# Full 128x128 stationary tiles in two attention cores and in the choice of keys

## The chip, the cores and the metric

The kernel runs on one core of one Trainium2 chip. The metric is the device time of one execution in microseconds (us). A core has TensorE (PE; its weight loads are shown apart as PEld), VectorE (DVE), ScalarE (ACT), GpSimd (POOL) and SyncE (SP), which issues most transfers. Each engine works through its own list of instructions in order and waits on semaphores for the others.

## The reference, cut to what matters

Two transformer blocks run over 512 positions of width 1024. The change lies in the second block, in its two attention branches:

```
z = h @ w_in
a_q, a_k, a_v, i_q, i_k, i_w, c_q, c_kv, k_r, g = split_cols(z, IN_SIZES)

# branch A: sparse attention, 8 heads of width 64, one key and one value shared by all heads
dots  = einsum('bqhd,bsd->bqhs', iq, ik) * 64 ** -0.5          # 4 indexer heads of width 64
score = einsum('bqh,bqhs->bqs', iw, relu(dots))                # causal
sel   = top_k(score, 128)
p     = softmax(q @ k_sel * 64 ** -0.5 + bias)                 # over the chosen keys
y_a   = p @ v_sel

# branch B: 8 heads, query and key of width 64 + 32 (rope), value of width 64
logits = (qn . kn + qr . kr) * 96 ** -0.5                      # causal
y_b    = softmax(logits) @ v
```

Queries are taken in blocks of 128 positions (qb = 0 to 3), which see 128 (qb + 1) keys.

## The kernel before, in words

A matrix product on PE takes a stationary tile (contraction rows on partitions x output rows) and a moving one. Most products are split: weights and activations are each held as a high and a low part, and `mm3` (L288) issues high x high, high x low and low x high. The products of the attention cores are plain float products through `mm` (L293), and each is carried out as two passes, which the trace shows as two weight loads and two matmuls (x2). The profile gives a stationary tile as rows*columns: 64*128, 96*128, 128*64 or 128*128.

The changed stage is `branch_stage` (from L1944). In order on PE:

- The input products z (`z_ch` weights) for 8 tiles, then the sparse queries `AQ`, then the gates (`gt`). A generator, `best_pe`, is advanced from within these products. It turns the token values (`tokens`) and issues the indexer's score products `dots`, one for each of 4 heads and each of qb = 1 to 3 (qb = 0 sees only 128 keys and needs no choice). The indexer's queries `IQ` and key `IK` lie in slots of the tile `QM`: two heads share one 128-partition tile, so head h uses partitions 64 (h % 2) to 64 (h % 2) + 63, and the key is there twice, once for each half. `best_dve` adds up the weighted scores and finds the 128 largest in 16 rounds of `max` and `match_replace` for every qb; the result is `Msel`, a bf16 mask.
- The values of branch B, `VB` (a 128x512 tile for each block of 128 keys, 64 columns a head).
- The MLA core: 32 items (8 heads, 4 query blocks). Before a pair of heads, `heads_pe` makes the pair's queries and keys, which ACT copies and DVE turns (rope) into `QM` and `KM`.
- The DSA core: 32 items (4 query blocks, 8 heads), with the output products of branch B (`branch_b_pe`) advanced by one step for each item, from the third item on, 24 steps in all.

Both cores are objects of the class `Core`. Item i passes `scores` (PE: in the DSA core first a mask product, identity x `Msel`, then query x key), `soft` (DVE: bias and row maximum), `exps` (ACT), `weigh` (DVE), `turns` (PE: transposes of 128x128, L816), `turned` (ACT: copy to `sq`) and `values` (PE: values as the stationary tile, 128 keys x 64 columns, over `sq`). `Core.run` sets a fixed order: in one step every engine works on its parts of different items, on PE `scores(i)`, `turns(i - 3)`, `values(i - 4)`. The output of a value product lies in partitions 0 to 63 of a PSUM bank; `mla_close_act` and `dsa_close_act` copy it to the lower or upper half of a pair tile.

On POOL the stage has only the powers for norms: `power("z")`, `power("cq")`, `power("ckv")`. PE's `spread` products wait for them. DVE's `z_evac` scales the z tiles out of PSUM; tile 6 holds the sparse key `AK`, once in each half of the partitions.

Of the kernel before, what the change touches and what calls it, by code (L numbers as in the profile page):

```python
# [214 lines left out]
def program(nc, ins, out):  # L215
# [3 lines left out]
    with ctx:  # L219
# [1724 lines left out]
        def branch_stage():  # L1944
            QOFF = [0, 128, 384, 768]
            ph = ExitStack()
            GT, Msel = sb("GT", [P, 16, S], F32, ph), sb("Msel", [P, 1280], BF16, ph)
            identb = sb("identb", [P, P], BF16, ph)
            AK, AV = sb("AK", [P, S], F32, ph), sb("AV", [P, 4, 64], F32, ph)
            AQ, IW = sb("AQ", [P, 4, S], F32, ph), sb("IW", [P, 4, 4], F32, ph)  # L1950
            SC = [sb(f"sc{i}", [P, S], F32, ph) for i in range(2)]
            pm = ExitStack()
            QM, KM, VB = sb("QM", [P, 4, S], F32, pm), sb("KM", [P, 4, S], F32, pm), sb("VB", [P, 4, S], F32, pm)
# [5 lines left out]
            stat_a = sb("stat_a", [P, 8 * 4 * 3], F32, pa)  # L1959
            pa.close()  # L1960
            B2.insert(0, sb("B20", [P, 2, H, 64], F32, pa))
            pa.close()
# [7 lines left out]
            stat_b, mx8 = extra[:, 0:96], [extra[:, 96:104], extra[:, 104:112]]  # L1970
# [45 lines left out]
            def best_pe():  # L2016
                for _ in range(3):
                    yield
                b = acc_bank("tokens", [(act_done, "tokens")])
                pe.wait_ge(*dve_done["zt", 7])  # L2020
                for tb in range(4):
                    tok = pe.e.transpose(b[:, tb * P:(tb + 1) * P], tmp[3][:, tb * P:(tb + 1) * P], ident[:, :])
                tok.then_inc(*core_done.up("tokens"))
                yield
                for qb in range(1, 4):
                    N = P * (qb + 1)
                    for h in range(4):
                        rows = slice(64 * (h % 2), 64 * (h % 2) + 64)
# [65 lines left out]
            def mla_item(h, qb):  # L2094
                N, x, j = P * (qb + 1), 2 * ((h // 2) % 2) + h % 2, h // 2
                b = OB["mla"][h % 2]
                return {"N": N, "in1": causal[:, S - N:S], "in1_ready": lambda: [pool_done["causal"]], "scale": 96.0 ** -0.5,
                        "comps": [(QM[0:96, x, qb * P:(qb + 1) * P], KM[0:96, x, 0:N])],
                        "ready": lambda: [act_done["mq", j, h % 2], dve_done["mrot", j, h % 2], act_done["kr"], act_done["mk", j, h % 2]],
                        "v": lambda kb: (VB[:, kb, 64 * h:64 * h + 64], act_done["vb", 3]), "bank": b,  # L2100
                        "dest": banks[b][0:64, qb * P:(qb + 1) * P], "opens": (act_done, ("mo", h)) if qb == 0 else None}

            def dsa_item(h, qb):
                N, n = P * (qb + 1), 2 * qb + h // 4
                rows = slice(64 * (h % 2), 64 * (h % 2) + 64)
# [136 lines left out]
            def mla_close_act(i):  # L2242
                if i and i % 8 == 0:
                    split_b_act(i // 8 - 1)
                if i % 4 == 3:
                    h = i // 4
                    act.wait_ge(*core_done["mla", "V", i])
                    if h // 2 > 1:
                        act.wait_ge(*dve_done["yb", h // 2 - 2])
                    act.e.activation(pair_buf[h // 2 % 2][64 * (h % 2):64 * (h % 2) + 64, :], banks[OB["mla"][h % 2]][0:64, :],  # L2250
                                     ACT.Copy).then_inc(*act_done.up(("mo", h)))

            def mla_close_dve(i):
                if i and i % 8 == 0:
# [17 lines left out]
            def dsa_close_act(i):  # L2272
                if i and i % 4 == 0:
                    split_a_act(i // 4 - 1)
                if i % 4 == 3:
                    n = i // 4
                    o = split_a(n)[2]
                    from_ = banks[OB["dsa"][n % 2]][:, :].rearrange("p (j x q) -> p j x q", j=2, x=2)
                    act.wait_ge(*core_done["dsa", "V", i])
                    act.wait_ge(*(dve_done["ya", n - 2] if n > 1 else dve_done["yb", 3]))  # L2280
                    act.e.activation(o[0:64], from_[0:64, :, 0, :], ACT.Copy).then_inc(*act_done.up())
                    act.e.activation(o[64:P], from_[0:64, :, 1, :], ACT.Copy).then_inc(*act_done.up(("do", n)))

            def dsa_close_dve(i):
                if i and i % 4 == 0:
# [39 lines left out]
                     lambda m: [(dve_done, ("x", "f2", m))])  # L2325


            def times_norm(dst, b, *key):
                dve.wait_ge(*act_done["rb", "z"])
                dve.e.tensor_tensor(dst, b[:, :], RB, ALU.mult).then_inc(*dve_done.up(key))  # L2330

            def z_evac(m):
                dve.wait_ge(*gemm_done["z", m])
                dst = [CQ[:, 0, :], CQ[:, 1, :], CQ[:, 2, :], tmp[0][:, :], IQ[:, 0, :], IQ[:, 1, :], AK[:, :], tmp[3][:, :]][m]
                times_norm(dst, bank(("z", m)), "zt", m)
# [4 lines left out]
            def vector():  # L2340
# [11 lines left out]

                def aq_evac(m):
                    dve.wait_ge(*gemm_done["aq", m])
                    times_norm(AQ[:, m, :], bank(("aq", m)), "aq", m)

                beside_gemm(dve, "z_ch", 0, DT, 2, aq_evac)
                dve.within[:] = [top]
# [1 line left out]

                def gt_evac(m):
                    dve.wait_ge(*gemm_done["gt", m])
                    times_norm(GT[:, m, :], bank(("gt", m)), "gt", m)

                beside_gemm(dve, "gates", 0, DT, 8, gt_evac)
                dve.within[:] = []
# [33 lines left out]
            def z_act(m):  # L2400
                if m == 3:
                    act.wait_ge(*dve_done["zt", 3])
                    act.e.activation(IK[0:64, :], tmp[0][0:64, :], ACT.Copy).then_inc(*act_done.up())
                    act.e.activation(IK[64:P, :], tmp[0][0:64, :], ACT.Copy).then_inc(*act_done.up("ik"))
# [284 lines left out]
```

## Time and profile before

| | |
|---|---|
| median of 3 runs | 2220.16 us (2215.21 to 2221.14) |
| span of the profiled execution | 2216.4 us |
| PE busy | 2123.1 us, 96% |
| weight loads (PEld) | 1654.6 us, 75% |
| DVE busy | 1344.6 us, 61% |
| ACT busy | 870.1 us, 39% |
| POOL busy | 154.3 us, 7% |

The profiled execution is one run; its span is counted from its first to its last instruction, and the run's own device time is not given apart from the three above. The span lies 3.8 us below their median. Busy time of PE is the union of its matmuls' modelled durations, so that matmuls following one another closely overlap, and a busy PE is not PE at its peak.

### The profile page before, as it was taken

What the parts mean: (1) busy time and instruction counts of PE and PEld (TensorE: products, weight loads), DVE (VectorE), ACT (ScalarE), POOL (GpSimd) and SP (SyncE); (2) the same over time, 40 slices, a digit from 0 to 9 for tenths busy, and PEclk for the clock granted to TensorE, in tenths of its full rate; (3) what the DMA queues carried; (4) which work ended last, traced back from release to release, by engine and by line L of the source; (5) the groups of instructions that cost most, each with busy time, mean ns of one, the idle gap of its engine ahead of it and who ended that gap; (6) DMA issues with size and microseconds to landing.
All of it is one profiled execution on the core that took longest, in us unless ns stands there. A gap on an engine that the chain in (4) does not pass through costs nothing.

```text
span 2216.4 us, 26169 instructions
## 1 busy us (share of the span) xinstructions
PE 2123.1 (96%) x10573; PEld 1654.6 (75%) x10575; DVE 1344.6 (61%) x2281; ACT 870.1 (39%) x1453; POOL 154.3 (7%) x101
## 2 busy tenths in 40 slices
PE   5999999999999999899999999999989999999998
PEld 4755768888887876677887887776755588888886
DVE  7697478847834566647764566458775465623632
ACT  4455534423423255534432443332365433412421
POOL 0464100000010000020000001000000000000000
PEclk9999999999999999999999999999999999999998
DMA  8343226565521221012333233222113022332331
GB/s 304 126 148 99 77 67 202 189 208 172 181 92 58 77 67 39 29 48 82 103 107 106 90 95 120 67 76 77 49 47 124 20 80 91 95 96 94 95 95 67
DMA packets 67112, 225.01 MB, mean 102 GB/s; under 512 B 7216, under 2 KB 8112, under 8 KB 66992
## 3 DMA queue, kind: packets, MB, share of 16 engines
q1 hardware_dynamic: 64112, 218.11, 30.6%
q10 hardware_dynamic: 2880, 5.24, 0.6%
q8 instruction: 83, 1.36, 0.3%
q14 instruction: 37, 0.30, 0.0%
HBM read 215.98 MB, written 7.34 MB: 101 GB/s over the span
## 4 chain that ended last, share of the span: by engine, by line
PE 84%; DVE 9%; ACT 3%; issue 2%; DMA 0%; POOL 0%; SPq 0%; DVEq 0%; POOLq 0%; ACTq 0%
PE bank L289 23%; PE bank L291 22%; PE bank L290 22%; PE bank L294 15%; PE bank L816 1%; DVE wlo L329 1%; ACT whi L316 1%; DVE sc L2084 1%; DVE steps L2082 1%; DVE tmp L545 1%; DVE Hl L550 1%; ACT pr L789 1%; DVE pr L781 0%; POOL small L525 0%; DMA XT<-in_xT 0%
## 5 line engine op out<-in xcount | busy, mean ns | idle before, releaser
L289 PE MATMUL bank<-Hh,whi 128*128 128x512 f32 x1632 | 653.8, 401 | 25.2 <-DVE wlo L329 9.9
L290 PE MATMUL bank<-Hl,whi 128*128 128x512 f32 x1632 | 640.4, 392 | 0.0
L291 PE MATMUL bank<-Hh,wlo 128*128 128x512 f32 x1632 | 640.4, 392 | 0.0
L329 DVE TENSOR_TENSOR wlo<-stg,whi 128x1024 fp32r<-128x1024 f32 (+1 forms) x299 | 358.8, 1205 | 427.6 <-ACT whi L316 427.0
L316 ACT ACTIVATE whi<-stg 128x1024 fp32r<-128x1024 f32 (+1 forms) x309 | 313.1, 1025 | 424.9 <-PE bank L291 418.3
L289 PEld LDWEIGHTS bank<-Hh,whi 128*128 128x128 f32 x1632 | 309.6, 190 | 105.6 <-issue 19.4
L291 PEld LDWEIGHTS bank<-Hh,wlo 128*128 128x128 f32 x1632 | 309.4, 190 | 66.0
L290 PEld LDWEIGHTS bank<-Hl,whi 128*128 128x128 f32 x1632 | 310.1, 190 | 61.0 <-issue 0.2
L289 PE MATMUL bank<-HIDh,whi 128*128 128x512 f32 x352 | 141.9, 403 | 0.0
L291 PE MATMUL bank<-HIDh,wlo 128*128 128x512 f32 x352 | 140.0, 398 | 0.0
L290 PE MATMUL bank<-HIDl,whi 128*128 128x512 f32 x352 | 138.6, 394 | 0.0
L1111 DVE SCALAR_TENSOR_TENSOR bank<-U,vec,bank 128x512 f32<-128x512 f32 x145 | 109.6, 756 | 5.1
L432 POOL TENSOR_TENSOR part<-sq 128x512 f32<-128x512 f32 x7 | 9.0, 1291 | 1357.3 <-ACT sq L427 1339.8
L291 PE MATMUL bank<-HID2h,wlo 128*128 128x512 f32 x256 | 102.1, 399 | 0.0
L290 PE MATMUL bank<-HID2l,whi 128*128 128x512 f32 x256 | 100.9, 394 | 0.0
L289 PE MATMUL bank<-HID2h,whi 128*128 128x512 f32 x256 | 100.5, 393 | 0.0
L1446 DVE SCALAR_TENSOR_TENSOR tmp<-bank,vec,tmp 128x511 f32<-128x511 f32 x88 | 65.9, 748 | 49.1 <-ACT tmp L1400 49.1
L629 DVE CUSTOM_DVE_ANT_0 raw<-raw,c_act 128x1024 f32<-128x1024 f32 x72 | 87.2, 1219 | 5.8 <-DMA raw<-in_mod_w 5.6
L1400 ACT ACTIVATE tmp<-bank,vec 128x512 f32<-128x512 f32 x88 | 67.7, 770 | 55.0 <-PE bank L291 55.0
L294 PE MATMUL bank<-U,dtap 128*128 128x512 f32 x186 | 85.1, 616 | 1.2 <-ACT dtap L1251 1.2
L291 PEld LDWEIGHTS bank<-HIDh,wlo 128*128 128x128 f32 x352 | 66.1, 188 | 15.6
L290 PEld LDWEIGHTS bank<-HIDl,whi 128*128 128x128 f32 x352 | 66.2, 188 | 15.0
(296 smaller groups left out, 2757.0 us busy)
## 6 DMA issues: line engine op xcount, KB each, us to landing
raw<-in_mod_w SPq DMA_DIRECT2D x96, 512.0 KB, 4.4
stg<-in_ffn_in SPq DMA_DIRECT2D x88, 512.0 KB, 3.8
stg<-in_ff SPq DMA_DIRECT2D x64, 512.0 KB, 3.5
stg<-in_ffn_out SPq DMA_DIRECT2D x40, 512.0 KB, 3.6
stg<-in_cm_w SPq DMA_DIRECT2D x24, 512.0 KB, 3.8
stg<-in_gates SPq DMA_DIRECT2D x16, 512.0 KB, 3.5
stg<-in_z_ch SPq DMA_DIRECT2D x12, 512.0 KB, 3.6
bias_kept<-out_b ACTq DMA_DIRECT2D x20, 256.0 KB, 2.1
```

Source lines behind the costliest of these rows:

```text
L289: pe.e.matmul(out_, l[0], r[0], start=start, stop=False, skip_group_check=True)
L290: pe.e.matmul(out_, l[0], r[1], start=False, stop=False, skip_group_check=True)
L291: return pe.e.matmul(out_, l[1], r[0], start=False, stop=stop, skip_group_check=True)
L294: return pe.e.matmul(out_, l, r, start=start, stop=stop, skip_group_check=True)
L316: act.e.activation(whi[j % NW][:, 0:n * c], stg[j % NSTG][:, 0:n * c], ACT.Copy).then_inc(*w_hi.up(j))
L329: hand.e.tensor_tensor(wlo[j % NW][:, 0:n * c], stg[j % NSTG][:, 0:n * c], whi[j % NW][:, 0:n * c].bitcast(F32), ALU.subtract).then_inc(*m ...
L545: dve.e.scalar_tensor_tensor(tmp[t % 4][:, :], x_tile(t), gain, r[:, :], ALU.mult, ALU.mult).then_inc(*dve_done.up(("hm", ver, t)))
L550: dve.e.scalar_tensor_tensor(Hl[:, t, :], tmp[t % 4][:, :], shift, Hh[:, t, :].bitcast(F32), ALU.add, ALU.subtract).then_inc(*dve_done.up( ...
L629: dve.e.tensor_tensor_reduce(raw[j % NRAW][:, :], raw[j % NRAW][:, :], c_act[:, :], 1.0, 0.0, ALU.mult, ALU.add, modv[:, a:a + 1]).then_in ...
L1111: dve.e.scalar_tensor_tensor(a[:, :] if k < CONV - 1 else C[:, t, :], U[:, t, k:k + S], vcol("cm_dw", 8 * k + t), a[:, :], ALU.mult, ALU.a ...
L1400: act.e.activation(at_, bank((("up", l, j), m))[:, :], ACT.Identity, bias=column(bcol + c), scale=column(w3 + 88 + c)).then_inc(*act_done. ...
L1446: dve.e.scalar_tensor_tensor(o[:, 1:S], from_[:, 0:S - 1], column(w3 + 44 + c), o[:, 1:S], ALU.mult, ALU.add).then_inc(*dve_done.up())
```

## The change

All products of the two cores and of the indexer now have a stationary tile that fills the array's columns, and those with 64 contraction rows get 128. (The scores of the MLA core keep their 96 rows.)

- Keys. `IK` and `AK` each become two tiles, one for even and one for odd heads. The one for even heads has the key in partitions 0 to 63 and zeros in 64 to 127, the other the reverse. The product takes the whole 128-partition query tile with two heads in it; the zeros cancel the other head. POOL writes the four halves of zeros once, behind `power("z")`; the score products of indexer and DSA core wait for the last one.
- Values. In the MLA core the stationary tile holds the values of both heads of the pair (128 columns), in the DSA core the shared value twice. The output fills 128 partitions, of which the half that belongs to the head is copied.
- `z_evac(6)` writes its two halves into the two key tiles with two DVE operations in place of one; ACT copies the token values twice.
- The identity in bf16, the indexer's head weights `IW` and the statistics `stat_a` move into parts of an existing tile (`steps_t`).

```diff
-            AK, AV = sb("AK", [P, S], F32, ph), sb("AV", [P, 4, 64], F32, ph)
-            AQ, IW = sb("AQ", [P, 4, S], F32, ph), sb("IW", [P, 4, 4], F32, ph)
+            AK, AV = [sb(f"AK{x}", [P, S], F32, ph) for x in range(2)], sb("AV", [P, 4, P], F32, ph)
+            AQ = sb("AQ", [P, 4, S], F32, ph)
...
-            IQ, IK, CQ = QM[:, 0:2, :], QM[:, 2, :], VB
+            IQ, IK, CQ = QM[:, 0:2, :], [QM[:, 2, :], QM[:, 3, :]], VB
...
+                        pe.wait_ge(*pool_done["zeros"])
                         pe.wait_ge(*dve_done["zt", 5])
-                        mm(banks[5][:, 0:N], IQ[rows, h // 2, qb * P:(qb + 1) * P], IK[rows, 0:N], True, True).then_inc(
+                        mm(banks[5][:, 0:N], IQ[:, h // 2, qb * P:(qb + 1) * P], IK[h % 2][:, 0:N], True, True).then_inc(
...
-                act.e.activation(AV[:, :, :], from_[:, :, 0:64], ACT.Copy).then_inc(*act_done.up("av"))
+                act.e.activation(AV[:, :, 0:64], from_[:, :, 0:64], ACT.Copy).then_inc(*act_done.up())
+                act.e.activation(AV[:, :, 64:P], from_[:, :, 0:64], ACT.Copy).then_inc(*act_done.up("av"))
...
-                        "v": lambda kb: (VB[:, kb, 64 * h:64 * h + 64], act_done["vb", 3]), "bank": b,
-                        "dest": banks[b][0:64, qb * P:(qb + 1) * P], "opens": (act_done, ("mo", h)) if qb == 0 else None}
+                        "v": lambda kb: (VB[:, kb, P * j:P * j + P], act_done["vb", 3]), "bank": b,
+                        "dest": banks[b][:, qb * P:(qb + 1) * P], "opens": (act_done, ("mo", h)) if qb == 0 else None}
...
-                        "comps": [(AQ[rows, h // 2, qb * P:(qb + 1) * P], AK[rows, 0:N])],
-                        "ready": lambda: [dve_done["aq", h // 2], dve_done["zt", 6], dve_done["idb"]] + (
+                        "comps": [(AQ[:, h // 2, qb * P:(qb + 1) * P], AK[h % 2][:, 0:N])],
+                        "ready": lambda: [dve_done["aq", h // 2], dve_done["zt", 6], dve_done["idb"], pool_done["zeros"]] + (
...
-                        "dest": banks[b][0:64, (h % 4) * P:(h % 4 + 1) * P], "opens": (act_done, ("do", n)) if h % 4 == 0 else None}
+                        "dest": banks[b][:, (h % 4) * P:(h % 4 + 1) * P], "opens": (act_done, ("do", n)) if h % 4 == 0 else None}
...
+                if m == 6:
+                    times_norm(AK[0][0:64, :], bank(("z", m)), [], slice(0, 64))
+                    times_norm(AK[1][64:P, :], bank(("z", m)), [("zt", m)], slice(64, P))
+                    return
...
                 power("z")
                 pool.wait_ge(*norm_done["sum", "z"])
+                for x, other in ((0, slice(64, P)), (1, slice(0, 64))):
+                    pool.wait_ge(*pool_done.now)
+                    pool.e.memset(IK[x][other, :], 0.0).then_inc(*pool_done.up())
+                    pool.wait_ge(*pool_done.now)
+                    pool.e.memset(AK[x][other, :], 0.0).then_inc(*pool_done.up(*(["zeros"] if x else [])))
+                pool.wait_ge(*pool_done.now)
                 power("cq")
```

## Rows read from the trace of the kernel before

**Rows 1.** The chain of waits that ended last, by engine.

```profile
PE 84%; DVE 9%; ACT 3%; issue 2%; DMA 0%; POOL 0%; SPq 0%; DVEq 0%; POOLq 0%; ACTq 0%
```

**Rows 2.** By stretch: us; PE, PEld, DVE, ACT, POOL busy; clock; DMA.

```profile
1440.00:1475.00 35.00, 34.53 (x171) 28.91 (x170) 16.91 (x25) 11.11 (x16) 3.02 (x3) 0.95 0.24 73
1475.00:1517.00 42.00, 42.00 (x170) 30.16 (x169) 30.40 (x71) 13.63 (x21) 0.00 (x0) 1.00 0.24 77
1517.00:1600.00 83.00, 75.52 (x301) 57.88 (x300) 67.62 (x131) 21.05 (x28) 0.00 (x0) 0.94 0.19 59
1622.70:1641.55 18.85, 17.56 (x93) 11.71 (x93) 13.50 (x42) 12.76 (x34) 0.00 (x0) 1.00 0.18 57
1684.00:1780.00 96.00, 94.86 (x450) 56.58 (x452) 45.54 (x150) 45.05 (x127) 0.00 (x0) 1.00 0.18 61
```

**Rows 3.** Timeline of PE in the DSA core: start us, us, instructions merged.

```profile
1729.49 0.91 PE L294 MATMUL bank<-AK,AQ 64*128 64x384 f32 x2
1730.33 0.55 PE L816 MATMUL bank<-ident,sc 128*128 128x128 f32 x3
1730.81 0.65 PE L294 MATMUL bank<-sq,AV 128*64 128x128 f32 x4
1731.39 0.50 PE L289 MATMUL bank<-Hh,whi 128*128 128x512 f32 x1
...
1732.20 0.34 PE L294 MATMUL bank<-Msel,identb 128*128 128x384 bf16 x1
1732.46 0.91 PE L294 MATMUL bank<-AK,AQ 64*128 64x384 f32 x2
```

**Rows 4.** Timeline of PE in the MLA core.

```profile
1643.95 1.09 PE L294 MATMUL bank<-sq,VB 128*64 128x128 f32 x8
1644.96 0.49 PE L294 MATMUL bank<-KM,QM 96*128 96x128 f32 x2
1645.29 0.38 PE L816 MATMUL bank<-ident,sc 128*128 128x128 f32 x2
1645.60 0.43 PE L294 MATMUL bank<-sq,VB 128*64 128x128 f32 x2
```

**Rows 5.** Timeline of PE at the indexer's first product.

```profile
1476.35 0.70 PE L294 MATMUL bank<-QM 64*128 64x256 f32 x2
1476.98 0.50 PE L289 MATMUL bank<-Hh,whi 128*128 128x512 f32 x1
```

**Rows 6.** Timeline of PE in the first block's attention core, full value tiles.

```profile
814.97 0.52 PE L816 MATMUL bank<-ident,pr 128*128 128x128 f32 x3 [1.05 <-DVE pr L808]
815.32 0.61 PE L294 MATMUL bank<-aT,Vt 128*128 128x128 f32 x4
815.69 0.48 PE L289 MATMUL bank<-Hh,whi 128*128 128x512 f32 x1
816.00 0.39 PE L290 MATMUL bank<-Hl,whi 128*128 128x512 f32 x1
```

**Rows 7.** Groups by line: busy us, mean ns of one, idle before.

```profile
L294 PEld LDWEIGHTS bank<-aT,Vt 128*128 128x128 f32 x160 | 21.8, 202 | 0.1
...
L294 PEld LDWEIGHTS bank<-sq,AV 128*64 128x64 f32 x160 | 16.6, 136 | 4.9 <-issue 4.0
```

**Rows 8.** PE's waits in the MLA core: us in total, times, longest.

```profile
PE bank L289 <- ACT QM L2203: 1.0, 1, 1.0
```

**Rows 9.** Timeline of PE, bf16 products ahead of a split product.

```profile
1141.53 0.63 PE L294 MATMUL bank<-Tb,step 128*128 128x32 bf16 x19
1142.01 0.48 PE L289 MATMUL bank<-HIDh,whi 128*128 128x512 f32 x1
```

**Rows 10.** POOL at the cq power (timeline), and its additions (groups by line).

```profile
1456.81 1.01 POOL L525 TENSOR_TENSOR small<-small 128x4 f32<-128x4 f32 x1 [14.59 <-DVE small L505]
...
L436 POOL TENSOR_TENSOR part<-part,sq 128x512 f32<-128x512 f32 x28 | 38.4, 1370 | 126.4 <-ACT sq L427 123.6 <-ACT sq L1243 1.8
```

**Rows 11.** Timeline of PE in the first block, scores of two components.

```profile
821.36 0.92 PE L294 MATMUL bank<-Kt,Qt 64*128 64x384 f32 x4
```

More of the change, by code:

```diff
@@ L1947, in branch_stage @@
             GT, Msel = sb("GT", [P, 16, S], F32, ph), sb("Msel", [P, 1280], BF16, ph)
-            identb = sb("identb", [P, P], BF16, ph)
-            AK, AV = sb("AK", [P, S], F32, ph), sb("AV", [P, 4, 64], F32, ph)
-            AQ, IW = sb("AQ", [P, 4, S], F32, ph), sb("IW", [P, 4, 4], F32, ph)
+            AK, AV = [sb(f"AK{x}", [P, S], F32, ph) for x in range(2)], sb("AV", [P, 4, P], F32, ph)
+            AQ = sb("AQ", [P, 4, S], F32, ph)
             SC = [sb(f"sc{i}", [P, S], F32, ph) for i in range(2)]
@@ L1958, in branch_stage @@
             B2 = [sb(f"B2{qb}", [P, 2 * qb + 2, H, 64], F32, pa) for qb in (3, 2, 1)][::-1]
-            stat_a = sb("stat_a", [P, 8 * 4 * 3], F32, pa)
             pa.close()
@@ L1967, in branch_stage @@
             YBh, YBl, YAh, YAl = Hh[:, 0:4, :], Hl[:, 0:4, :], Hh[:, 4:8, :], Hl[:, 4:8, :]
-            IQ, IK, CQ = QM[:, 0:2, :], QM[:, 2, :], VB
+            IQ, IK, CQ = QM[:, 0:2, :], [QM[:, 2, :], QM[:, 3, :]], VB
             extra = steps_t[:, 2, :].bitcast(F32)
-            stat_b, mx8 = extra[:, 0:96], [extra[:, 96:104], extra[:, 104:112]]
+            stat_b, stat_a, mx8 = extra[:, 0:96], extra[:, 112:208], [extra[:, 96:104], extra[:, 104:112]]
+            identb, IW = steps_t[:, 3, 0:P], steps_t[:, 3, P:P + 32].bitcast(F32).rearrange("p (t h) -> p t h", t=4)
             RB = steps_t[:, 0:2, :].rearrange("p x q -> p (x q)").bitcast(F32)
@@ L2027, in best_pe @@
                     for h in range(4):
-                        rows = slice(64 * (h % 2), 64 * (h % 2) + 64)
                         open_bank(5, [(act_done, ("relu", qb, h))])
                         pe.wait_ge(*act_done["ik"])
+                        pe.wait_ge(*pool_done["zeros"])
                         pe.wait_ge(*dve_done["zt", 5])
-                        mm(banks[5][:, 0:N], IQ[rows, h // 2, qb * P:(qb + 1) * P], IK[rows, 0:N], True, True).then_inc(
+                        mm(banks[5][:, 0:N], IQ[:, h // 2, qb * P:(qb + 1) * P], IK[h % 2][:, 0:N], True, True).then_inc(
                             *core_done.up(("dots", qb, h)))
@@ L2099, in mla_item @@
                         "ready": lambda: [act_done["mq", j, h % 2], dve_done["mrot", j, h % 2], act_done["kr"], act_done["mk", j, h % 2]],
-                        "v": lambda kb: (VB[:, kb, 64 * h:64 * h + 64], act_done["vb", 3]), "bank": b,
-                        "dest": banks[b][0:64, qb * P:(qb + 1) * P], "opens": (act_done, ("mo", h)) if qb == 0 else None}
+                        "v": lambda kb: (VB[:, kb, P * j:P * j + P], act_done["vb", 3]), "bank": b,
+                        "dest": banks[b][:, qb * P:(qb + 1) * P], "opens": (act_done, ("mo", h)) if qb == 0 else None}
             def dsa_item(h, qb):
                 N, n = P * (qb + 1), 2 * qb + h // 4
-                rows = slice(64 * (h % 2), 64 * (h % 2) + 64)
                 b = OB["dsa"][n % 2]
@@ L2249, in mla_close_act @@
                         act.wait_ge(*dve_done["yb", h // 2 - 2])
-                    act.e.activation(pair_buf[h // 2 % 2][64 * (h % 2):64 * (h % 2) + 64, :], banks[OB["mla"][h % 2]][0:64, :],
-                                     ACT.Copy).then_inc(*act_done.up(("mo", h)))
+                    rows = slice(64 * (h % 2), 64 * (h % 2) + 64)
+                    act.e.activation(pair_buf[h // 2 % 2][rows, :], banks[OB["mla"][h % 2]][rows, :], ACT.Copy).then_inc(*act_done.up(("mo", h)))
             def mla_close_dve(i):
@@ L2281, in dsa_close_act @@
                     act.e.activation(o[0:64], from_[0:64, :, 0, :], ACT.Copy).then_inc(*act_done.up())
-                    act.e.activation(o[64:P], from_[0:64, :, 1, :], ACT.Copy).then_inc(*act_done.up(("do", n)))
+                    act.e.activation(o[64:P], from_[64:P, :, 1, :], ACT.Copy).then_inc(*act_done.up(("do", n)))
             def dsa_close_dve(i):
@@ L2325, in tensor, with times_norm @@
                      lambda m: [(dve_done, ("x", "f2", m))])
-            def times_norm(dst, b, *key):
+            def times_norm(dst, b, key, rows=slice(0, P)):
                 dve.wait_ge(*act_done["rb", "z"])
-                dve.e.tensor_tensor(dst, b[:, :], RB, ALU.mult).then_inc(*dve_done.up(key))
+                dve.e.tensor_tensor(dst, b[rows, :], RB[rows, :], ALU.mult).then_inc(*dve_done.up(*key))
             def z_evac(m):
                 dve.wait_ge(*gemm_done["z", m])
-                dst = [CQ[:, 0, :], CQ[:, 1, :], CQ[:, 2, :], tmp[0][:, :], IQ[:, 0, :], IQ[:, 1, :], AK[:, :], tmp[3][:, :]][m]
-                times_norm(dst, bank(("z", m)), "zt", m)
+                if m == 6:
+                    times_norm(AK[0][0:64, :], bank(("z", m)), [], slice(0, 64))
+                    times_norm(AK[1][64:P, :], bank(("z", m)), [("zt", m)], slice(64, P))
+                    return
+                dst = [CQ[:, 0, :], CQ[:, 1, :], CQ[:, 2, :], tmp[0][:, :], IQ[:, 0, :], IQ[:, 1, :], None, tmp[3][:, :]][m]
+                times_norm(dst, bank(("z", m)), [("zt", m)])
                 if m == 3:
@@ L2354, in aq_evac @@
                     dve.wait_ge(*gemm_done["aq", m])
-                    times_norm(AQ[:, m, :], bank(("aq", m)), "aq", m)
+                    times_norm(AQ[:, m, :], bank(("aq", m)), [("aq", m)])
                 beside_gemm(dve, "z_ch", 0, DT, 2, aq_evac)
@@ L2362, in gt_evac @@
                     dve.wait_ge(*gemm_done["gt", m])
-                    times_norm(GT[:, m, :], bank(("gt", m)), "gt", m)
+                    times_norm(GT[:, m, :], bank(("gt", m)), [("gt", m)])
                 beside_gemm(dve, "gates", 0, DT, 8, gt_evac)
@@ L2402, in z_act @@
                     act.wait_ge(*dve_done["zt", 3])
-                    act.e.activation(IK[0:64, :], tmp[0][0:64, :], ACT.Copy).then_inc(*act_done.up())
-                    act.e.activation(IK[64:P, :], tmp[0][0:64, :], ACT.Copy).then_inc(*act_done.up("ik"))
+                    act.e.activation(IK[0][0:64, :], tmp[0][0:64, :], ACT.Copy).then_inc(*act_done.up())
+                    act.e.activation(IK[1][64:P, :], tmp[0][0:64, :], ACT.Copy).then_inc(*act_done.up("ik"))
                     act.wait_ge(*dve_done["kr"])
```

## The prediction

> **What bounds the kernel now.** I read the page first, for the chain of waits, then busy time by stretch, then the timeline of TensorE alone in the stage that is changed, then the groups by line and the list of waits. The chain that ended last lies on PE for 84% [rows 1], so the first question of any edit is what it does to PE's order of work, and only the second what it does to the others. The stretches [rows 2] cut the changed stage into parts with different limits. From 1475 to 1517 us (second part of the input products, with eight of the indexer's score products among them) PE is busy 42.00 of 42.00 us. From 1517 to 1600 us DVE has 67.6 of 83 us and PE has holes: this is the choice of keys, where DVE's chain of maxima leads. One pair of heads of the MLA core, 1622.70 to 1641.55 us, has PE at 17.56 of 18.85 us, DVE at 13.50, ACT at 12.76. The sparse core (DSA), 1684 to 1780 us, has PE at 94.9 of 96 us, DVE and ACT at 45 each. [...]
>
> PE busy is not PE at work, because the ends of products are modelled, so I compare ends: the end of a row is its start plus its us, and the distance between two ends, less what the later products take in a dense stream, is time lost between them. Stream times: one pass of 128 columns takes 0.11 (value products x8 in 1.09, x2 in 0.43: six more in 0.66) [rows 4]; a 512-column pass of a split (high/low) product 0.22 to 0.23 (end 816.17 to end 816.39) [rows 6]; a float product is two passes at half that speed, 0.32 a pass at 384 columns and 0.43 at 512, in proportion to the 0.11 [rows 4].
>
> One item of the sparse core [rows 3]:
> - score (64 rows) to transposes: ends 1730.40 and 1730.88, 0.48 for three transposes of 0.11: lost 0.15.
> - transposes to values (64 columns): ends 1730.88 and 1731.46, 0.58 for four of 0.11: lost 0.14.
> - values to the first product of branch B: ends 1731.46 and 1731.89, 0.43 for 0.23: lost 0.20.
> - mask to score: ends 1732.54 and 1733.37, 0.83 for two passes of 0.32: lost 0.19.
>
> One item of the MLA core [rows 4]: values to the next score, ends 1645.04 and 1645.45, 0.41 for 0.22, lost 0.19. Score (96 rows) to transposes, ends 1645.45 and 1645.67, 0.22 for 0.22: nothing lost. Transposes to values, 1645.67 to 1646.03, 0.36 for 0.22: lost 0.14. The indexer [rows 5]: from the 64-row product back to the main products, ends 1477.05 and 1477.48, 0.43 for 0.23: lost 0.20.
>
> So time goes exactly where a stationary tile with 64 rows or 64 columns stands next to one that is full, and none where 96 rows meet 128. What full tiles do in the same place is shown by the first block's attention [rows 6]: transposes, then value products with a 128*128 tile, then split products end at 815.49, 815.93 and 816.17. That is 0.44 for four passes and 0.24 for one of 0.23: nothing is lost, though type and bank change too.
>
> **The change part by part.**
>
> *MLA values, 64 to 128 columns.* 32 items, each enters and leaves the 64-column tile once: 32 x (0.14 + 0.19) = 10.6 us of PE. The product itself: 0.44 for four at full width [rows 6] against 0.11 each at 64 columns [rows 4], so no charge. The weight load grows from 136 to 202 ns [rows 7]; beside a full product it stays covered, as the 0.1 us of idle time before the 160 full loads says. Lost again: with PE faster, what is late next? In one pair of heads PE streams scores 5 x 0.86 = 4.3 (2,560 columns, two passes), 20 transposes and 40 value passes at 0.11 = 6.6, and 15 head products at 0.23 = 3.5: 14.4 us, plus 8 x 0.33 = 2.6 lost at the tiles: 17.0 of 18.85. The remaining 1.8 are waits, among them one on the readers of the head products' bank [rows 8]. After the change DVE's 13.5 and ACT's 12.8 stand beside 14.4 rather than 17.0. The pair is still PE's, but DVE must also turn the new heads in one lump (six operations), and the order is fixed on every engine. I give back a quarter, 0.65 of 2.6 a pair: 8.0 us saved in the stage. Bounds: 10.6 (no new wait) and 1.5 (the pair falls only towards the floor of its waits, priced under the rivals).
>
> *DSA scores to 128 rows, values to 128 columns.* 32 items.
> - Mask to score: 0.19 each. What remains is a load of 128 columns behind a short mask product. The nearest row is a 32-column bf16 product before a full split product, ends 1142.16 and 1142.49, 0.33 for 0.23 [rows 9]: 0.10 stays. With 128 columns of mask (8 items) I let 0.06 stay, else 0.02: 8 x 0.13 + 24 x 0.17 = 5.1. Bounds: 2.9 (0.10 stays everywhere) and 6.1.
> - Score to transposes: 32 x 0.15 = 4.8, less a few thousandths each: 4.6.
> - Transposes to values: 32 x 0.14 = 4.5.
> - Values to branch B, which stands behind 24 of the items: 24 x 0.19 = 4.6. The other 8 go on to a mask; no row here separates that step, it lies between 0 and 0.2, I take 0.1: 0.8.
>
> Sum 19.6. DVE and ACT have over 40% free even in 76 us; I give back 0.8 for odd waits: 18.8. Bounds 15 and 21.
>
> *Indexer scores to 128 rows.* 12 products, each with an exit of 0.20 and an entry priced as mask to score, 0.19. The first 8 lie in the stretch where PE has no hole: 8 x 0.39 = 3.1. The last 4 lie where DVE leads: 0, at best 1.6.
>
> *Costs.* The padding needs four POOL writes of 64x512. They stand behind the z power and ahead of the cq power, before which POOL idles 14.59 us [rows 10]. The trace has no such write; the nearest POOL row, a 128x512 addition, takes 1.37: four make 5.5 us, and even with a semaphore between them they end near 1449, before the power at 1456.8 and long before the first indexer product at 1476 that waits for them. Cost 0; it begins above 3.3 us a write, and then PE's spread product is late, with the input products behind it. The evacuation of z tile 6 becomes two on DVE, at a place where DVE is busy 16.9 of 35 us [rows 2]; ACT, with 13.6 of 42 busy, copies the token values once more, ahead of a weight split and of the first relu. I bound each from above by the larger POOL addition, 1.37 [rows 10], and take 0 for both. The added waits on the zeros stand in PE's queue ahead of products that also wait for later events. Moving the identity, the head weights and the statistics to other memory changes no instruction.
>
> [...] In the first block's attention four 64-row passes of 384 columns end in 0.92 us [rows 11], while in the sparse core two such passes take 0.91 [rows 3]: there two components in different row halves run at the same time, here each score stands alone between mask and transposes. [...]
>
> **Sum.** 8.0 + 18.8 + 3.1 = 29.9 us, off the profiled execution's span of 2216.4: 2186.5. The median of the runs is 2220.16, 3.8 above that span, so 2190.
>
> **Rivals.**
> 1. *The MLA core becomes bound by its helpers* (0.12). The head preparation, ACT's copy, DVE's turn, then PE's third product in the same bank, sets the pair's length, and only some 0.2 a pair is won there. For: a wait on the bank's readers is in the list already [rows 8], and DVE's load is 13.5. Against: 14.4 + 1.8 of waits is still above 13.5. Then 18.8 + 3.1 + 0.7 = 22.6: 2197.6.
> 2. *The step from mask to score stays* because the type changes as well as the tile (0.06). For: mask to score is the one changed step with a type change into a float product. Against: 0.10 at 32 columns [rows 9]. Then 29.9 - 5.1: 2195.4.
> 3. *The other side: wide loads aren't covered* (0.03). If each of the 320 value loads stood in the open with its 0.20 [rows 7] behind a product of only 0.11, 64 us would come and 30 go: 2220 + 34 = 2254. It decides for slower from 0.10 a load. Against: the full-width value products of the first block stream at 0.11 [rows 6].
> 4. *The change doesn't do what it says* (0.03): the loss belongs to the order of operations and not to the tile, and stays. Then 2220. Against: rows 6 have the same order without loss.
>
> **How the numbers follow.** Forecast 0.76, rivals 0.12, 0.06, 0.03, 0.03. A difference of 0.3% (6.7 us) is what can be told from none. Faster: 0.76 + 0.12 + 0.06 = 0.94; same 0.03 (rival 4); slower 0.03 (rival 3). Low end: all of 10.6 + 21 + 4 = 35.6, 2184.6, with 1.6 for the runs' spread: 2183. High end: rival 1 with its 2197.6 and a further 4 (bounds of the DSA sum): 2202. That leaves out some 0.15.
>
> **What would show it.** Right: DSA shrinks from 96 to about 77 us; a pair of heads from 18.85 to about 16.8; 1475 to 1517 to about 39; value loads near 200 ns at unchanged ends of 0.11 a pass; no idle time before loads of the value and score groups; the stages before and behind unchanged. Wrong: a pair of heads above 18; ends between value passes above 0.13; losses of 0.15 or more left at any of the four steps; a spread product that waits for POOL near 1457.

## The result: 27.6 us less in the medians, 23.7 in the profiled executions

| | before | changed |
|---|---|---|
| median of the runs | 2220.65 us | 2193.05 us (2191.39 to 2194.54) |
| ratio of the runs | | 0.9884 (95% interval 0.9871 to 0.9897) |
| span of the profiled execution | 2216.4 us | 2192.7 us |
| chain of waits, PE / DVE / ACT | 84 / 9 / 3% [rows 1] | 82 / 10 / 4% |

Predicted were 2190 us and a range of 2183 to 2202. To see where the time went I cut both traces at the same instructions: first to ninth indexer product, MLA core (first score product to end of the last value product), DSA core (from there to the end of its last value product), and the second block's first feed-forward part of the stage behind (first product of `w_out` to first product of `ff2`). By stretch (us; PE, PEld, DVE, ACT, POOL busy; granted clock; DMA share and GB/s), the kernel before:

```profile
1476.35:1541.12 64.77, 64.77 (x269) 49.03 (x268) 50.26 (x114) 18.93 (x27) 0.00 (x0) 1.00 0.23 74
1611.29:1685.02 73.73, 66.80 (x350) 43.79 (x350) 51.03 (x158) 49.35 (x126) 0.00 (x0) 1.00 0.19 62
1685.02:1776.98 91.96, 91.02 (x431) 53.70 (x433) 44.34 (x148) 42.93 (x123) 0.00 (x0) 1.00 0.18 64
1799.30:1934.99 135.69, 135.69 (x610) 111.83 (x608) 76.95 (x93) 54.19 (x74) 8.57 (x6) 1.00 0.31 97
```

and the changed one:

```profile
1477.46:1539.62 62.16, 61.88 (x270) 50.25 (x268) 49.81 (x113) 19.25 (x27) 0.00 (x0) 1.00 0.26 77
1607.99:1678.08 70.09, 60.00 (x351) 44.63 (x352) 50.55 (x158) 48.53 (x126) 0.00 (x0) 0.98 0.21 66
1678.08:1751.96 73.88, 72.16 (x432) 55.05 (x433) 43.43 (x148) 43.32 (x123) 0.00 (x0) 1.00 0.23 79
1774.28:1911.41 137.13, 137.13 (x609) 112.83 (x608) 76.94 (x93) 54.16 (x74) 8.58 (x6) 0.99 0.30 96
```

So 2.6 us come from the indexer's first eight products, 3.6 from the MLA core, 18.1 from the DSA core, 24.3 in all. The remainder is for the most part not the change's own: the changed execution is 1.2 us late when it reaches the stage, gains 1.8 between the ninth indexer product and the branch B values, and loses 1.4 in the stretch last shown. The latter two go, all but some 0.5 of the 1.8 (see the indexer's experiment), with the granted clock. In the rows below it is 0.50, for 3.4 or 6.8 us at a time; in the fall from 1833.70 a 512-column pass of a split product ends 0.43 us after the one before (1834.61, 1835.04, 1835.47), not 0.23. Before, the falls lie in and behind the choice of keys, with PE busy for 5.50 of 6.80 and 3.16 of 3.40 us:

```profile
1552.70:1559.50 6.80, 5.50 (x10) 3.31 (x11) 4.51 (x8) 1.84 (x3) 0.00 (x0) 0.50 0.27 77
1590.20:1593.60 3.40, 3.16 (x8) 2.49 (x9) 3.26 (x8) 0.00 (x0) 0.00 (x0) 0.50 0.30 77
```

and in the changed kernel, where the second fall is absent and two others stand, one at the start of the MLA core and one between feed-forward products:

```profile
1833.70:1837.10 3.40, 3.40 (x10) 2.62 (x9) 0.38 (x1) 0.00 (x0) 1.25 (x1) 0.50 0.50 154
1608.40:1611.80 3.40, 3.40 (x7) 1.63 (x6) 2.99 (x13) 2.33 (x6) 0.00 (x0) 0.50 0.29 77
1550.40:1557.20 6.80, 4.36 (x8) 2.83 (x9) 3.62 (x6) 2.99 (x5) 0.00 (x0) 0.50 0.27 77
```

Ends of rows, read as in the prediction, show what became of each step. PE in the changed DSA core (answers to [rows 3]):

```profile
1710.00 0.34 PE L294 MATMUL bank<-Msel,steps 128*128 128x384 bf16 x1
1710.17 0.81 PE L294 MATMUL bank<-AK,AQ 128*128 128x384 f32 x2
1710.82 0.38 PE L816 MATMUL bank<-ident,sc 128*128 128x128 f32 x2
1711.04 0.61 PE L294 MATMUL bank<-sq,AV 128*128 128x128 f32 x4
1711.40 0.48 PE L289 MATMUL bank<-Hh,whi 128*128 128x512 f32 x1
...
1682.29 0.23 PE L294 MATMUL bank<-Msel,steps 128*128 128x128 bf16 x1
1682.36 0.44 PE L294 MATMUL bank<-AK,AQ 128*128 128x128 f32 x2
```

Mask to score 0.64 for two passes of 0.32, score to transposes 0.22 for two of 0.11, then 0.45 for four and 0.23 for one: 0.19, 0.15, 0.14 and 0.20 have become 0.01 at most. Only with 128 columns of mask does something stay, 0.28 for 0.22, the 0.06 that I had let stand. In the MLA core (answers to [rows 4]), ends 1641.01, 1641.24, 1641.45, 1641.68, all steps of 0.21 to 0.23 for 0.22:

```profile
1639.95 1.06 PE L294 MATMUL bank<-sq,VB 128*128 128x128 f32 x8
1640.85 0.39 PE L294 MATMUL bank<-KM,QM 96*128 96x128 f32 x2
1641.07 0.38 PE L816 MATMUL bank<-ident,sc 128*128 128x128 f32 x2
1641.29 0.39 PE L294 MATMUL bank<-sq,VB 128*128 128x128 f32 x2
```

The indexer (answers to [rows 5]) goes back to the main products with 0.25 for 0.23:

```profile
1477.46 0.59 PE L294 MATMUL bank<-QM 128*128 128x256 f32 x2
1477.71 0.59 PE L289 MATMUL bank<-Hh,whi 128*128 128x512 f32 x1
```

Value loads now take 192 ns instead of 136, with next to no idle time before them (groups by line, as [rows 7]):

```profile
L294 PEld LDWEIGHTS bank<-sq,VB 128*128 128x128 f32 x160 | 20.4, 192 | 1.4 <-issue 1.2 <-ACT sq L824 0.2
L294 PEld LDWEIGHTS bank<-sq,AV 128*128 128x128 f32 x160 | 20.4, 192 | 0.2
```

POOL's four writes of zeros (timeline, the last of them) end 12 us before the power for cq at 1458.02:

```profile
1445.28 0.52 POOL L2464 MEMSET AK<- 64x512 f32 x1
```

### The profile page after: what moved, and what is told of

Its sections match the earlier page's. It is cut to its first block, busy times and chain, and to the rows that moved or that the text cites. A ratio compares the mean times of both kernels' runs of the same rounds, so it can differ in the third digit from the quotient of the medians.

```text
span 2192.7 us, 26176 instructions
## 1 busy us (share of the span) xinstructions
PE 2092.9 (95%) x10573; PEld 1658.9 (76%) x10575; DVE 1343.8 (61%) x2282; ACT 869.7 (40%) x1454; POOL 156.5 (7%) x105
## 4 chain that ended last, share of the span: by engine, by line
PE 82%; DVE 10%; ACT 4%; issue 3%; POOL 0%; DMA 0%; SPq 0%; DVEq 0%; POOLq 0%; ACTq 0%
PE bank L289 22%; PE bank L291 22%; PE bank L290 22%; PE bank L294 14%; DVE wlo L329 1%; ACT whi L316 1%; DVE sc L2084 1%; PE bank L816 1%; DVE steps L2082 1%; DVE tmp L545 1%; DVE Hl L550 1%; ACT pr L789 1%; DVE pr L781 0%; POOL small L525 0%; ACT GT L2429 0%
## 5 line engine op out<-in xcount | busy, mean ns | idle before, releaser
L329 DVE TENSOR_TENSOR wlo<-stg,whi 128x1024 fp32r<-128x1024 f32 (+1 forms) x299 | 358.8, 1205 | 427.8 <-ACT whi L316 427.2
L316 ACT ACTIVATE whi<-stg 128x1024 fp32r<-128x1024 f32 (+1 forms) x309 | 313.1, 1025 | 425.6 <-PE bank L291 417.6
```

Of the source, the lines that this page charges most:

```text
L316: act.e.activation(whi[j % NW][:, 0:n * c], stg[j % NSTG][:, 0:n * c], ACT.Copy).then_inc(*w_hi.up(j))
L329: hand.e.tensor_tensor(wlo[j % NW][:, 0:n * c], stg[j % NSTG][:, 0:n * c], whi[j % NW][:, 0:n * c].bitcast(F32), ALU.subtract).then_inc(*m ...
```

## The experiments

Each stage's length in a trace repeats to 0.1 us from kernel to kernel where its code is the same and the clock doesn't fall (the DSA core takes 73.88 to 73.91 us in the ten kernels that have it as changed), so the stretches decide. The run times, which scatter by 2 to 9 us within one kernel, stand beside them.

### One part undone at a time

```diff
# MLA values
-  "v": (VB[:, kb, P * j:P * j + P], ...), "dest": banks[b][:, ...]
+  "v": (VB[:, kb, 64 * h:64 * h + 64], ...), "dest": banks[b][0:64, ...]
```

> The changed kernel with the MLA values back to 64 columns (output in partitions 0 to 63). Theory (time is lost where a 64-column tile stands next to a full one, and in the MLA core most of what was won turned into new waits): the core grows from 70.1 us (first score to last value product) back to the 73.7 of before, the losses of 0.19 and 0.14 an item return, DVE and ACT waits of PE shrink; time about 2196.7, 3.6 above the changed kernel. Rival (each item's 0.33 counts in full, and the smaller gain seen in the MLA core came from something else in the change, such as the moved statistics or the shared weights of the heads): 10.6 more, 2203.6.

Measured: 2200.62 us, ratio to before 0.9921 (0.9908 to 0.9934). The MLA core takes 74.49 us, 4.40 more than in the changed kernel; the clock fall at its start is the same in both:

```profile
1608.17:1682.66 74.49, 68.20 (x351) 44.50 (x351) 51.11 (x158) 49.18 (x126) 0.00 (x0) 0.98 0.19 62
```

The tile itself is the cause, and its net worth in this core is 4.4 of the 10.6 us that the losses at its edges add up to: 0.8 more than expected, 6.2 less than the rival said. The median grew by 7.6 us, twice what I expected; see below the fourth experiment.

```diff
# DSA values
-  "v": (AV[:, kb, :], ...), "dest": banks[b][:, ...]
+  "v": (AV[:, kb, 0:64], ...), "dest": banks[b][0:64, ...]
```

> The changed kernel with the DSA values back to 64 columns. Theory: the DSA core grows by 32 x 0.14 + 24 x 0.19 + 8 x 0.1 = 9.9 us, time about 2203. Rival (once one of the two kinds of narrow tile is there, most of the loss is there, since PE would have had to wait at these places anyway): under 5, 2198.

Measured: 2204.86 us, ratio 0.9934 (0.9920 to 0.9948); DSA core 82.20 us, 8.32 more.

```profile
1679.85:1762.05 82.20, 80.91 (x431) 53.67 (x432) 44.00 (x148) 43.13 (x123) 0.00 (x0) 1.00 0.21 71
```

```diff
# DSA scores
-  (AQ[:, h // 2, ...], AK[h % 2][:, 0:N])
+  (AQ[64 * (h % 2):64 * (h % 2) + 64, h // 2, ...], AK[h % 2][64 * (h % 2):64 * (h % 2) + 64, 0:N])
```

> The changed kernel with the DSA scores back to 64 rows (query and key read from their own half of the partitions). Theory: mask to score 5.1 and score to transposes 4.6 come back, 9.7 in the DSA core, time about 2202.7. Rival (mask to score costs by its change of type, whatever the tile): only 4.6 come back, 2197.6.

Measured: 2203.84 us, ratio 0.9931 (0.9917 to 0.9944); DSA core 83.34 us, 9.46 more. Mask to score is lost by the tile and not by the type: the ends lie 0.84 apart again, for two passes of 0.32.

```profile
1680.45:1763.79 83.34, 81.99 (x432) 54.24 (x433) 44.00 (x148) 43.05 (x123) 0.00 (x0) 1.00 0.20 70
```

```profile
1716.98 0.34 PE L294 MATMUL bank<-Msel,steps 128*128 128x384 bf16 x1
1717.25 0.91 PE L294 MATMUL bank<-AK,AQ 64*128 64x384 f32 x2
```

The two halves of the DSA core add up: 8.32 + 9.46 = 17.8 against 18.1 for both.

```diff
# indexer
-  IQ[:, h // 2, ...], IK[h % 2][:, 0:N]
+  IQ[64 * (h % 2):64 * (h % 2) + 64, h // 2, ...], IK[h % 2][64 * (h % 2):64 * (h % 2) + 64, 0:N]
```

> The changed kernel with the indexer's scores back to 64 rows. Theory of the prediction (only the first 8 products count, the last 4 stand where DVE leads): 3.1 us, time 2196.2. Rival (all 12 count, since in the stretch 1517 to 1602 of before DVE's chain begins behind these products too): 4.6, 2197.6, with the stretch from the last but three of the 12 products to the first head product growing by 1 to 2 us.

Measured: 2199.23 us, ratio 0.9908 (0.9894 to 0.9922). First to ninth product 64.77 us, to the hundredth as before, 2.61 more than changed. From the ninth to the branch B values it is longer too, 61.8 against 60.0, as before, and the fall at 1590 us is back. Nine of the twelve kernels with the full tile take 60.0 there, at a mean clock of 0.94; the other three have one fall or more in addition and take 61.3 to 62.9. Two of those have the clock of the narrow tile, 0.92, and take 61.3 and 61.4, so some 0.5 us of the 1.8 belong to the last four products themselves. Whether the narrow tile also brings the fall about stays open. A by-product: here the MLA core has a clock of 1.00 throughout and takes 69.30, not 70.09, so the fall in the changed kernel costs some 0.8.

```profile
1476.23:1541.00 64.77, 64.77 (x269) 49.03 (x268) 50.23 (x114) 19.20 (x27) 0.00 (x0) 1.00 0.24 74
1611.19:1680.49 69.30, 58.66 (x351) 43.81 (x352) 50.41 (x158) 48.61 (x126) 0.00 (x0) 1.00 0.20 66
```

In the medians the four undoings cost 7.6, 11.8, 10.8 and 6.2 us, 36.4 together, where the whole change is worth 27.6. The stretches that they touch grew by 24.8, so the surplus lies outside them or in the spread from run to run: the undone DSA values, for one, reach the first indexer product 1.8 us later than the changed kernel, ahead of anything that was edited, and lose 1.6 more behind the DSA core (138.72 for 137.13) at a lower mean clock, 0.98 for 0.99. The medians show that each undoing costs time; they don't price it.

### 96 columns

```diff
-  VB[:, kb, P * j:P * j + P]                 AV[:, kb, :]
+  VB[:, kb, P * j:P * j + (P if h % 2 else 96)]    AV[:, kb, 0:P if h % 2 else 96]   # dest cut to 96 partitions
```

> The changed kernel with 96 instead of 128 columns in the value tiles of the even heads, in both cores (16 of 32 items each). Theory (what counts is whether the tile falls into the class of the full array, as the 96-row scores do): time as the changed kernel, 2193, ends of value passes 0.11 apart, no loss at their edges. Rival (any tile with fewer than 128 columns next to a full one loses time): 16 x (0.14 + 0.19) in the DSA core, 5.3 us, and some 1.8 in the MLA core: 2200.

Measured: 2194.33 us, ratio 0.9886 (0.9868 to 0.9905); MLA core 70.01, DSA core 73.72 us, no longer than with full tiles. Timeline of PE in the DSA core: ends 1706.49, 1706.93, 1707.16, that is 0.44 for four passes and 0.23 for one.

```profile
1706.11 0.38 PE L816 MATMUL bank<-ident,sc 128*128 128x128 f32 x2
1706.33 0.60 PE L294 MATMUL bank<-sq,AV 128*96 128x128 f32 x4
1706.68 0.48 PE L289 MATMUL bank<-Hh,whi 128*128 128x512 f32 x1
```

```profile
1673.43:1747.15 73.72, 72.10 (x434) 54.83 (x433) 43.38 (x148) 43.30 (x123) 0.00 (x0) 1.00 0.24 79
```

So the tile needn't be full: between one of 64 rows or columns and its neighbours 0.14 to 0.20 us were lost, between one of 96 and a full one nothing. Why the two sizes differ, no run shows; the class of tile that the expectation speaks of is my reading of these losses.

### Where the MLA core's other 6 us went

PE's waits there, from the list of waits over the whole core, sum to 7.6 us before and 10.7 after. The largest of the changed kernel's:

```profile
PE bank L289 <- issue: 3.0, 2, 2.6
PE bank L816 <- DVE sc L799: 3.0, 4, 1.2
PE bank L816 <- DVE steps L799: 1.8, 2, 1.6
PE bank L289 <- ACT QM L2202: 1.6, 1, 1.6
```

They stand around the preparation of a pair of heads: PE's third product, whose bank ACT and DVE must have read, and the next transposes, which want DVE's weighing (L799). In DVE's timeline the six operations of the turn and a weight split stand in one piece ahead of that weighing (the rows go on with maximum and weighing at 1658.25):

```profile
1651.35 1.22 DVE L329 TENSOR_TENSOR wlo<-stg,whi 128x1024 fp32r<-128x1024 f32 x1 [0.92 <-ACT whi L316]
1652.60 0.69 DVE L2212 TENSOR_TENSOR tmp<-bank,ROT 32x512 f32<-32x512 f32 x1
1653.32 0.69 DVE L2213 TENSOR_TENSOR tmp<-bank,ROT 32x512 f32<-32x512 f32 x1
...
1656.28 0.68 DVE L2215 TENSOR_TENSOR QM<-tmp 32x512 f32<-32x512 f32 x1
1657.00 1.23 DVE L329 TENSOR_TENSOR wlo<-stg,whi 128x1024 fp32r<-128x1024 f32 x1
```

The third product itself:

```profile
1654.12 0.48 PE L289 MATMUL bank<-CQh,whi 128*128 128x512 f32 x1 [2.58 <-issue]
```

It starts 0.11 us after DVE's second operation of the turn, the last one that reads the bank, has ended at 1654.01. The list puts this wait down to "issue", and the one of 1.6 us at the pair before to ACT; but there too the product starts at 1635.64, 0.11 behind the same DVE operation, when ACT had been done for 1.0 us. So it is DVE that PE waits for at both places.

```diff
-                    rotate(QM[...], banks[...], tmp[2 * x], tmp[2 * x + 1], ("mrot", j, x), ("mturn", j, x))
+                    dve.e.tensor_tensor(QM[64:96, ...], banks[...][64:96, :], ROT[64:96, :], ALU.mult) ...
```

> The changed kernel with one DVE operation instead of three for the turn (rope) of each MLA query tile, so two of three rope operations of the queries are left out. DVE loses 4 operations of 0.7 us a pair, 2.8 us. Theory of the lump: PE's waits behind the preparation (third product on the readers of its bank, next transposes on DVE) shrink by about 2 us in each of three preparations inside the core and 1 at the first: MLA core about 63 us, 2186. Rival (the waits belong to the loop over ACT): under 2 us.

Measured: 2191.5 us, ratio 0.9876 (0.9861 to 0.9892), with two of the three turning operations of each query tile left out. The MLA core takes 65.44 us, 4.65 less, not the 7 that I expected, and the time before its first score falls by 0.8. PE's waits in the core fall from 10.7 to 6.7 us, below the 7.6 of the kernel before. So DVE's work around the preparation is on the path; how much of the missing 6 us it is can't be read from this, since the kernel before wasn't run without these operations. The profiled execution gives 2.9 of this back in the choice of keys, at a clock of 0.89.

```profile
1610.81:1676.25 65.44, 59.36 (x351) 45.41 (x352) 41.80 (x143) 48.24 (x126) 0.00 (x0) 0.97 0.22 70
```

The other kernels tried to move the work instead of leaving it out. `lead_mla` was given the items (of 8) at which each part of the preparation is done:

```diff
-                    elif i % 8 == 6 and i < 24:
-                        heads(i // 8 + 1)
+                    elif i < 24:
+                        for part in range(3):        # two query products, key product
+                            if i % 8 == at[part]:
+                                heads(i // 8 + 1, part)
```

Spread, `at` = (4, 5, 6) on all engines:

> The changed kernel with the head preparation of the MLA core spread over three steps (first query product at item 4 of 8, second at 5, key product at 6) in place of all three at 6. Theory (what took the MLA core's gain is the lump of the preparation: PE's third product waits for the readers of its bank, 1.6 to 2.6 us a pair, and the next transposes for DVE, which is late by its turns, 1.6): the three preparations inside the core lose 2 to 3 us less each, MLA core 70.1 to about 63, time about 2186. Rival (the loop of transposes, copy, exponential, weighing, transposes over two steps sets the pace between preparations as well): the waits move, the core shortens by under 3 us, 2190 or more.

Measured: 2200.81 us, ratio 0.9921 (0.9903 to 0.9939), MLA core 73.60 us: slower by 3.5, the opposite of what I expected; PE's transposes wait 11.8 us for DVE's weighing, not 4.8. ACT's order reversed (exponential first):

> The changed kernel with ACT's order in the MLA core reversed: in each step the exponential of item i - 1 first, then the copy of the transposes of item i - 3. Theory of the lump: little changes, within 1.5 us of 2193. Rival (the loop transposes, copy, exponential, weighing, transposes binds because the exponential stands behind the copy): MLA core 2 to 5 us shorter, 2188 to 2191; if instead the copy is what PE needs first (the next transposes reuse the one bank), it is 1 to 4 us longer.

Measured: 2201.5 us, ratio 0.9921 (0.9906 to 0.9937), MLA core 76.22: 6.1 longer, beyond the bound of 4. The copy is what PE needs first: its transposes wait for it 9.3 us, in the changed kernel 0.5.

```profile
PE bank L816 <- ACT sq L824: 9.3, 11, 1.4
```

Then PE one item ahead of the helpers, (4, 4, 6) against (5, 5, 7):

> The changed kernel with the MLA head preparation staggered: PE makes the two query products at item 4 of 8 and the key product at 6, ACT and DVE take them at 5 and 7 (they did so in the same step as PE before). New theory (lock step: in the step of the preparation DVE and ACT wait for PE's product, then do 4.1 us of turns, and only then the row maximum, exponential and weighing for which PE's next transposes wait; spreading the parts made three such stalls of one, 73.6 us instead of 70.1): the wait on PE's product goes, the turns stay in one lump; MLA core about 67, time 2190. Rival (PE's bank wait was the loss, and in the spread kernel something else was added): 66 to 67 as well, but without a difference between this kernel and the next. Rival (DVE has simply too much work around the preparation): no gain, 70 or more.

Measured: 2210.28 us, ratio 0.9955 (0.9938 to 0.9973), MLA core 84.47. And (4, 5, 6) against (5, 6, 7):

> As the kernel before it, with PE's three parts at items 4, 5 and 6 and those of ACT and DVE at 5, 6 and 7. Theory of the lock step: each DVE lump is half as long and none waits for PE; MLA core about 65, time 2188. If DVE's load around the preparation is what counts, 70 as in the changed kernel; if three parts are bad in themselves, as in the spread kernel, 73.

Measured: 2200.64 us, ratio 0.9914 (0.9900 to 0.9929), MLA core 74.61. The theory of the lock step falls: both are slower than the changed kernel, by 14.4 and 4.5 us. The rows of the four kernels, in this order:

```profile
1608.47:1682.07 73.60, 60.89 (x351) 46.37 (x352) 50.75 (x158) 48.17 (x126) 0.00 (x0) 0.95 0.19 62
```

```profile
1608.71:1684.93 76.22, 62.15 (x351) 45.87 (x352) 50.68 (x158) 50.02 (x126) 0.00 (x0) 0.96 0.19 60
```

```profile
1604.41:1688.88 84.47, 67.16 (x351) 50.44 (x352) 50.90 (x158) 47.63 (x126) 0.00 (x0) 0.86 0.17 54
```

```profile
1610.42:1685.03 74.61, 63.38 (x351) 47.45 (x352) 50.89 (x158) 47.76 (x126) 0.00 (x0) 0.93 0.19 62
```

DVE's and ACT's loads are the same in all (50.7 to 50.9, 47.6 to 50.0), so order decides and not work. Part of the price is the clock. The granted clock is 0.95, 0.96, 0.86 and 0.93 in these four, 0.98 in the changed core, and PE's busy time for the same products is longer by 0.9, 2.2, 7.2 and 3.4 us; only the rest, 2.6, 4.0, 7.2 and 1.1 us, is added idle time. The last kernel is slow mainly by its clock, and whether its order would be as slow at an undisturbed clock isn't shown.

Two waits of DVE stand out. The one for ACT's high part of a weight (L329 on L316) sums to 2.4 us in the changed core and to 6.9, 3.4, 9.9 and 4.4 in the four. The other is at the fifth of the eight items, where DVE takes the low part of the finished pair's output (L2238, or L2252 where lines have moved), for which ACT must have made the high part at the end of its own step. It sums to 4.7 us in the changed core and to 10.0 and 7.2 in the two staggered ones, where the turns stand right behind it, but to 3.4 in the spread one. The slowest kernel's:

```profile
DVE Hl L2252 <- ACT Hh L2248: 10.0, 3, 4.3
DVE wlo L329 <- ACT whi L316: 9.9, 5, 3.4
```

That these waits cause the loss stays an argument: a low part taken one item later would test it, and wasn't tried. Two more kernels were built on the last one. The MLA values back to 64 columns:

> The kernel before it (all parts staggered) with the MLA values back to 64 columns. Theory (the full price of the narrow tile, 32 x 0.33 = 10.6 us, shows only when PE is not waiting for helpers): 7 to 10 us above the kernel before it, where the same undoing in the changed kernel cost 4.4. Rival (the tile's price in the MLA core is really about 4): 4.

Measured: 2200.92 us, ratio 0.9917 (0.9899 to 0.9935), MLA core 77.66: 3.05 more where I expected 7 to 10, a miss, and only 0.3 in the medians. The core without the narrow tile has the lower clock (0.93 against 0.96), so 3.05 is not the tile's price alone; and PE still had 11.2 us of idle time there, so that kernel had not freed PE from its helpers. And weighing before the row maximum:

> All parts staggered, and in the MLA core DVE weighs item i - 2 before it takes the row maximum of item i - 1 (the other way round now). Theory (PE's next transposes wait for the weighing, which stands behind a maximum of 0.4 to 0.8 us): 1 to 3 us shorter than the staggered kernel. Rival (weighing then waits for the exponential with the maximum behind it, which delays the exponential after it): same or longer by up to 5.

Measured: 2209.24 us, ratio 0.9953 (0.9938 to 0.9968), MLA core 82.71, 8.1 more: the rival, and beyond its bound of 5. DVE's wait for the exponential (L796 on L789) grew from 4.9 to 17.0 us. No version beat the changed kernel with the whole computation in it.

## Why the prediction was right, and which term was off

- *Time is lost where a 64 tile meets a full one.* Right: every step's loss vanished, and came back with the tile when one was undone.
- *DSA core, 18.8.* Measured 18.1: PE's busy time fell by 18.9, and 0.8 came back as idle time, as much as I had given back. By parts: scores 9.7 expected, 9.46 by undoing; values 9.9 expected, 8.32. The 0.06 that stays behind a short mask came out as such.
- *Indexer, 3.1.* Measured 2.6 for the first eight products; 0.3 us of the difference is idle time that PE didn't have there before.
- *MLA core, 8.0.* The mis-sized term: 3.6 in the profiled executions, 4.4 with the tile alone undone, and 4.4 (73.73 to 69.30, the undone indexer's core) where no clock fall disturbs it. A pair of heads, first head product to first head product, took 17.5 us for 18.8, not 16.8; the pair before it 16.3 for 18.0. I gave back a quarter of the 10.6; more than half went. In the undisturbed core PE's busy time fell by 8.1 us (66.80 to 58.66), and idle time rose by 3.7. So 3.7 us became new waits, where I had put 2.6, and 2.4 of the 10.6 never were in PE's busy time. My low bound of 1.5 doesn't fit rival 1 either, which left only 0.7. Halfway to rival 1 would have been nearer: DVE's and ACT's loads of 13.5 and 12.8 in a pair look like slack beside 14.4, but they come in lumps in a fixed order. The 2.4 may be losses ahead of products that wait for ACT or DVE in any case, which cost nothing; that is argued, not measured.
- *Costs.* Right: the writes of zeros took 0.52 us each where the bound was 1.37, and the second evacuation and copy left no trace.
- *Padding against row halves.* That padding gives up what [rows 11] show, two components at once in different row halves (four passes end in 0.92 us where two in [rows 3] take 0.91), cost nothing, since undoing it made the DSA core 9.46 us longer. Nor did the wider loads, 192 ns for 136: 0.2 us of idle time stand before the 160 of the DSA core, 1.4 before those of the MLA core.
- *Rivals.* 2 fell by the undone scores (mask to score lost 0.20 again with the type unchanged), 3 by loads of 192 ns under passes of 0.11, 4 by all of it. Rival 1 was half right.
- *The clock* was no term of the sum. One fall less behind the choice of keys and two more elsewhere are some +1.3, -0.8 and -1.4 in the profiled pair.

The sum against the execution's own span was 29.9; 23.7 came, and 27.6 in the medians, between which lies the scatter of the runs before (2215 to 2221). The three changed stretches are worth 24.3. That the median came within 3 us of the forecast is therefore luck in part: 5.6 us were missing in the stretches, most of them in the MLA core, and the medians gave some of it back.

## What to carry to other kernels

Look at the distances between the ends of neighbouring products, not at how busy TensorE is: an engine busy for 96% of its span held some 30 us of losses between its products (my estimate from the ends). Where products of 64 rows or columns are woven singly between full ones, pad them to the 128 of their neighbours, with zeros written once or a neighbour's data. Here it cost no product time: four value passes still end in 0.45 us, and the DSA core's loads, 192 ns instead of 136, have 0.2 us of idle time before them in all. Count the gain in full only where no other engine is near. In the DSA core, with DVE and ACT busy for 43 of 73.9 us, 18.1 of 19.6 us came; in the MLA core, whose helpers were busy for over two thirds of the time (50.6 and 48.5 of 70.1 us), in lumps, 4.4 of 10.6.

## What the runs showed of the hardware

- At 96 columns (128*96 value tiles in both cores) nothing was lost: the four passes behind the transposes end in 0.44 us, the split product behind them in 0.23, and one load takes 163 ns. At 96 rows neither: score to transposes 0.22 before (1645.45 to 1645.67) and 0.21 after the change (1641.24 to 1641.45).
- With 64 rows or columns the loss depended on the way, and it came back where one part was undone. Into 64 columns from transposes it was 0.14 us before, 0.15 with the values of either core undone. Out of 64 columns, into a 96-row score or a split product, it was 0.19 and 0.20 before, 0.20 and 0.20 undone. Into 64 rows from a mask product it was 0.19 before, 0.20 with the DSA scores undone; out of 64 rows into transposes 0.15 in both; out of the indexer's 64 rows into a split product 0.20 before.
- The granted clock was 0.50 for 3.4 us from 1833.7 us in the changed kernel, with PE busy for 3.40 of 3.40. Ahead of it PE made 24 passes with a single moving column each (norm sums, timeline below), which count as busy and took 2.6 us (ends 1830.18 to 1832.75), 0.11 each. The stretch of this fall was 1.4 us longer than before (137.13 for 135.69). All fourteen kernels have these passes, and twelve have a fall behind them (eleven take 137.1 us in that stretch, one 138.7); the kernel before and the one with ACT's order reversed have none and take 135.69 and 135.55. So the passes alone don't bring it about, and its cause stays open.

```profile
1830.02 0.95 PE L294 MATMUL bank<-ones,part 128*128 128x1 f32 x8
1830.82 1.93 PE L294 MATMUL bank<-ones,sq 128*128 128x1 f32 x16
```
